# One front phase per layer: opening, norm, 22 projections, low-rank norms, queries, keys and convolution share one phase, and twelve projected tiles pass through memory

## The reference

```python
cond = silu(c)
for l in range(2):
    ada = cond @ ada_w[l] + ada_b[l]              # shift, scale, gate, twice
    h = rms_norm(x, norm1_g[l]) * (1 + sc1) + sh1
    (a_b, a_c, a_x, m_cq, m_ckv, m_kr, s_u, s_v,
     r_q, r_k, r_v, r_g, gate_logits) = split(h @ w_in[l])
    # short conv:  a_b * causal_conv3(a_c * a_x)
    # attention:   q = rms(m_cq) @ w_uq, k,v = rms(m_ckv) @ w_ukv, k_rope = m_kr,
    #              q,k rms-normed per head and rotated; 4 heads of 96, causal softmax
    # spatial gating: gelu(s_u) * (tril(w_s) @ rms(gelu(s_v)) + b_s)
    # retention:   chunked, q,k rotated, silu(r_g) * head_norm(o)
    x = x + g1 * (sum_n sigmoid(gate_n) * (y_n @ w_branch[n])) @ w_o[l]
    h = rms_norm(x, norm2_g[l]) * (1 + sc2) + sh2
    x = x + g2 * channel_mixer(h)
```

## Time and profile before

| what | value |
| --- | --- |
| median of 3 runs | 6089.78 us (6085.6 to 6098.41) |
| profiled execution: time | 6089.61 us |
| profiled execution: span | 6087.8 us |
| busy share of the span: PE, PEld, DVE, ACT, POOL | 89%, 74%, 39%, 30%, 30% |
| mean granted clock of PE | 0.937 |

### The profile page before, as it was taken

How to read it: one execution, slowest core, us unless ns; L and a number is a source line. 1 busy time by engine, 2 the same in 40 slices (tenths; PEclk the granted TensorE clock), 3 DMA queues, 4 the chain that set the end, 5 groups by cost and what they waited for, 6 DMA issues and landing times. The chain is left out here.

```text
span 6087.8 us, 73881 instructions
## 1 busy us (share of the span) xinstructions
PE 5410.3 (89%) x29832; PEld 4520.1 (74%) x29833; DVE 2375.2 (39%) x2058; ACT 1834.3 (30%) x1499; POOL 1846.6 (30%) x506
## 2 busy tenths in 40 slices
PE   6788799979999887978998499999999999999995
PEld 4366577758777663746776498998989898898985
DVE  4453333322422535341111233433364335753356
ACT  2131111123222112211111133333354334643344
POOL 1311011114343322111111152342454254642533
PEclk8798899989999997989999599999999999999997
DMA  4000133323633710101112265555577557975568
GB/s 160 18 19 24 47 80 83 98 62 96 171 109 99 211 35 0 38 4 43 47 45 85 101 210 186 195 191 186 193 257 247 193 182 234 337 254 189 188 226 293
DMA packets 803244, 827.43 MB, mean 136 GB/s; under 512 B 18370, under 2 KB 731202, under 8 KB 802754
## 3 DMA queue, kind: packets, MB, share of 16 engines
q1 hardware_dynamic: 795122, 794.49, 40.8%
q0 software_dynamic: 4608, 16.78, 0.8%
q10 hardware_dynamic: 3408, 14.68, 0.6%
HBM read 780.79 MB, written 45.09 MB: 136 GB/s over the span
## 5 line engine op out<-in xcount | busy, mean ns | idle before, releaser
L1935 POOL TENSOR_TENSOR e_w_lo<-e_raw,e_w_hi 128x2048 fp32r<-128x2048 f32 x170 | 1073.2, 6324 | 1478.3 <-ACT e_w_hi L1873 1478.3
L252 POOL TENSOR_TENSOR w_lo<-w_raw,w_hi 128x1024 fp32r<-128x1024 f32 (+1 forms) x260 | 622.5, 2395 | 2349.7 <-ACT w_hi L247 2349.7
L258 PE MATMUL banks<-e_x_hi,e_w_hi 128*128 128x256 f32 x3584 | 1019.6, 284 | 35.0 <-issue 23.9
L259 PE MATMUL banks<-e_x_lo,e_w_hi 128*128 128x256 f32 x3584 | 1018.5, 284 | 0.0
L260 PE MATMUL banks<-e_x_hi,e_w_lo 128*128 128x256 f32 x3584 | 1018.4, 284 | 0.0
L271 PE MATMUL banks<-h_hi,w_hi 128*128 128x512 f32 x1984 | 806.0, 406 | 127.0 <-POOL w_lo L252 78.5
L1873 ACT ACTIVATE e_w_hi<-e_raw 128x2048 fp32r<-128x2048 f32 x340 | 648.5, 1912 | 541.4 <-PE banks L260 530.2
L272 PE MATMUL banks<-h_lo,w_hi 128*128 128x512 f32 x1984 | 777.9, 392 | 0.0
L258 PEld LDWEIGHTS banks<-e_x_hi,e_w_hi 128*128 128x128 f32 x3584 | 692.7, 193 | 38.3 <-issue 26.0
L259 PEld LDWEIGHTS banks<-e_x_lo,e_w_hi 128*128 128x128 f32 x3584 | 692.6, 193 | 0.0
L260 PEld LDWEIGHTS banks<-e_x_hi,e_w_lo 128*128 128x128 f32 x3584 | 692.4, 193 | 0.0
(11 more groups left out here) (298 smaller groups left out, 7884.1 us busy)
## 6 DMA issues: line engine op xcount, KB each, us to landing
e_raw<-in_moe_w_dram SPq DMA_DIRECT2D x510, 1024.0 KB, 5.1
w_raw<-in_ffn_w_dram SPq DMA_DIRECT2D x120, 512.0 KB, 3.9
w_raw<-in_w_in_dram SPq DMA_DIRECT2D x108, 512.0 KB, 4.1
f_ada_raw<-in_ada_w_dram SPq DMA_DIRECT2D x48, 512.0 KB, 4.7
g_ada_raw<-in_ada_w_dram SPq DMA_DIRECT2D x32, 512.0 KB, 3.8
e_io<-row_scratch SPq DMA_DIRECT2D x13, 1024.0 KB, 6.2
x_scratch<-x_res SPq DMA_DIRECT2D x24, 512.0 KB, 3.2
y_scratch<-e_io ACTq DMA_DIRECT2D x12, 1024.0 KB, 4.2
```

Of the source, the lines that this page charges most:

```text
L252: pool.tensor_tensor(m.w_lo[b][:, 0:kt, :], m.w_raw[b][:, 0:kt, :], m.w_hi[b][:, 0:kt, :].bitcast(F32), ALU.subtract).then_inc(s.lo_ready, 1)
L258: pe.matmul(out, wh, rh, start=first, stop=False)
L259: pe.matmul(out, wh, rl, start=False, stop=False)
L1935: eng.tensor_tensor(flat(w_lo[u]), flat(raw[n % RING]), flat(w_hi[u]).bitcast(F32), ALU.subtract).then_inc(lo_sem[u % 2], 1)
```

## The change

Steps 1 to 5 and step 7 become one `front_phase` per layer. What it does:

- **Order of blocks.** The low-rank q, kv and rope blocks come first (0 to 3), then the 12 blocks of spatial gating and retention (4 to 15), then C, X, B of the convolution twice (16 to 21). Blocks 0 and 1 are done half by half (`half_block`), from block 2 on both halves use PSUM banks 0 and 1, and each half is evicted by itself.
- **Between the halves.** PE has a step (`beside`) after each half of blocks 3 to 11: the low-rank norm at block 3, and for head n, at blocks 4+2n and 5+2n, up, sums, spread, rotation. ACT, DVE and POOL have the matching pieces between their roundings, evictions and rests.
- **Memory.** Blocks 4 to 15 are evicted to a stage of two tiles, and SP stores each to `row_scratch` (12 stores of 512 KB). `attention_phase` loads ten of them back into `m.z` while the heads are worked on, `sgu_phase` the last two.
- **Convolution.** Its products read PSUM directly on DVE (`evict` of blocks 16 to 21) and `convolve` runs on DVE; POOL has no part in it.
- **Norm.** Scale, rounding and rest are on 128x512 halves, 16 rounds of each, and the second half's reciprocal comes between rounds 7 and 8.
- **Opening.** The first set of rotation angles is worked out by DVE before the `ada` work; its sines are taken by ACT after the ninth transposing step; `part_sum` has four buffers and the weight tiles three. The second set comes at blocks 2 to 5.
- **Layer 1.** The loads of x are the phase's first DMAs; the weights, parameters and tables follow, and DVE's first scale also waits for the tables.

```diff
+def half_block(pe, m, b, half, bank, ready=None):
+    tok = slice(half * HALF, (half + 1) * HALF)
+    for k in range(KT):
+        if ready is not None:
+            pe.wait_ge(ready, KT * half + k + 1)
+        last = mm3(pe, m.ps[:, bank, :], m.w_hi[b][:, k, :], m.w_lo[b][:, k, :],
+                   m.h_hi[:, k, tok], m.h_lo[:, k, tok], k == 0, k == KT - 1)
+    return last
+FRONT = ([C_CQ, C_CQ + P, C_CKV, C_KR + QKR - P] + [C_SU + P * i for i in range(12)]
+         + [c + P * t for t in range(2) for c in (C_C, C_X, C_B)])
+# sync
+            def spill(j):
+                sp.wait_ge(s.evicted, ended(j, 1))
...
+            if first:
...
+                for j in range(NB):
+                    if j >= 3:
+                        sp.wait_ge(s.added, j - 2)
+                    sp.dma_start(wb[j % 3][:, :, :], w_view(a.ada_w[0], j * W, W)).then_inc((s.ada0, s.ada1, s.ada2)[j % 3], 16)
+                sp.wait_ge(s.reduced, 4)
+            else:
+                for k in range(KT):
...
+                    sp.dma_start(m.x[:, k, :], a.xs[P * k:P * k + P, :]).then_inc(x_in[k % 4], 16)
             for j in range(2):
+                load(j)
...
             if first:
                 for k in range(KT):
+                    sp.wait_ge(s.copied, KT + k + 1)
+                    sp.dma_start(a.xs[P * k:P * (k + 1), :], m.x[:, k, :]).then_inc(s.kept, 16)
+                sp.wait_ge(s.kept, 16 * KT)
+                sp.wait_ge(s.lo, 2 * KT)
+                sp.dma_start(pos_i[1][:, :], a.positions.rearrange("o s -> (o s)").partition_broadcast(P)).then_inc(s.p_in, 16)
+            else:
+                sp.dma_start(m.table[:, :, :], a.tables).then_inc(s.tab_in, 16)
+            for j in range(2, NFRONT):
+                load(j)
+                if SPILL0 <= j - 3 < CONV0:
+                    spill(j - 3)
+# tensor
+            for half in range(NHALF):
+                for j in range(2):
+                    pe.wait_ge(s.lo_ready, j + 1)
+                    half_block(pe, m, j, half, 4 * j + half, s.lo if j == 0 else None).then_inc(s.halves, 1)
...
+            for j in range(2, NFRONT):
+                pe.wait_ge(s.lo_ready, j + 1)
+                for half in range(NHALF):
+                    pe.wait_ge(s.evicted, ended(j - 1 if j > 2 else 0, half))
+                    half_block(pe, m, j % 2, half, half).then_inc(s.halves, 1)
+                    beside(j, half)
+# tensor, in beside(j, half): head n at blocks 4+2n and 5+2n
+                if step == 0:
...
+                        pe.wait_ge(s.sined, 2 * n)
+                    up(n)
+                elif step == 1:
+                    pe.wait_ge(s.q_squared, 2 * n + 2)
+                    sums(n)
+                elif step == 2:
+                    pe.wait_ge(s.q_inv, n + 1)
...
+                else:
+                    rotate(n)
+# scalar
+            for j in range(2, NFRONT):
+                if j + 1 < NFRONT:
+                    round_w(j + 1)
...
+                if j >= HEAD0 and n < NG and (j - HEAD0) % 2 == 0:
+                    head_in(n)
+                    head_root(n)
+# gpsimd
+            for j in range(2, NFRONT):
+                if j + 1 < NFRONT:
+                    rest_w(j + 1)
...
+                    turn(n - 1)
...
+                    cosines(n)
+# vector
+            else:
+                dve.wait_ge(s.root, 1)
+                invert(0)
+                dve.wait_ge(s.tab_in, 16)
+            for n in range(2 * KT):
+                if n == KT:
+                    invert(1)
+                scale(n)
+                if n:
+                    rest(n - 1)
+            rest(2 * KT - 1)
...
+            for j in range(2, NFRONT):
...
+                evict(j, 0)
+                if first and j == 2:
...
+                    angle(1)
...
+                if ahead and (j - HEAD0) % 2 == 1:
+                    head_norm(head)
+                evict(j, 1)
+                if first and j == 2:
+                    fold(1)
...
+                if ahead and (j - HEAD0) % 2 == 0:
+                    dve.wait_ge(s.q_root, head + 1)
+                    dve.reciprocal(inv_rms[:, :], inv_rms[:, :]).then_inc(s.q_inv, 1)
+                if ahead and (j - HEAD0) % 2 == 1:
+                    head_sine(head)
...
+                if j >= CONV0 and (j - CONV0) % 3 == 1:
+                    convolve((j - CONV0) // 3)
 def build(nc, a):
...
-        opening_phase(nc, m, a)
         for l in range(DEPTH):
-            param_phase(nc, m, a, l)
-            norm_project_phase(nc, m, a, l, C_B, 10, C_KR + QKR - P)
-            conv_lora_phase(nc, m, l)
-            qk = qk_phase(nc, m, l)
-            attention_phase(nc, m, l, qk)
-            project_phase(nc, m, a, l, C_SU, 12)
-            sgu_phase(nc, m, l)
+            qk = front_phase(nc, m, a, l)
+            attention_phase(nc, m, a, l, qk)
+            sgu_phase(nc, m, a, l)
             retention_phases(nc, m, l)
```

More of the change, by code:

```diff
@@ L787, in flat @@
     def flat(t):
         return t.rearrange("p a n -> p (a n)")
-    with phase(nc, "up", "rope_in", "q_in", "squared", "summed", "root", "inv", "spread", "normed", "turned",
-               "cosed", "sined", "done") as (block, s):
+    names = ["squared", "totals", "root", "inv", "scaled", "hi", "lo", "raw0", "raw1", "hi_ready", "lo_ready", "halves", "evicted",
+             "st0", "st1", "ws_in", "prm_in", "ws_turned",
+             "l_squared", "l_summed", "l_root", "l_inv", "l_spread", "l_done",
+             "up", "rope_in", "q_in", "q_squared", "q_summed", "q_root", "q_inv", "q_spread", "normed", "q_turned",
+             "cosed", "sined", "done", "acc"]
@@ new lines, in _ @@
+            act.activation(rstd[:, :, :], m.ps[:, 6:8, :], ACT.Sqrt, bias=cst[:, K_EPS:K_EPS + 1], scale=1.0 / D).then_inc(s.root, 1)
+            for j in range(2):
+                round_w(j)
+            for half in range(NHALF):
+                for k in range(KT):
+                    n = KT * half + k
+                    act.wait_ge(s.scaled, n + 1)
+                    act.activation(m.h_hi[:, k, half * HALF:(half + 1) * HALF], tmp[n % 3][:, :], ACT.Identity,
+                                   bias=m.small[:, B + k:B + k + 1]).then_inc(s.hi, 1)
@@ new lines, in _ @@
+            round_w(2)
+            for j in range(2, NFRONT):
+                if j + 1 < NFRONT:
+                    round_w(j + 1)
+                if j == HEAD0 - 1:
+                    act.wait_ge(s.evicted, ended(2, 1))
+                    act.activation(l_sq[:, :, :].rearrange("p t n -> p (t n)"), zt(m, 0, 3), ACT.Square).then_inc(s.l_squared, 1)
+                    act.wait_ge(s.l_summed, 1)
+                    for q, n in ((0, QL), (1, P)):
+                        r = slice(2 * GR * q, 2 * GR * (q + 1))
+                        act.activation(inv_rms[r, :], m.ps[r, 6, :], ACT.Sqrt, bias=cst[r, K_EPS:K_EPS + 1], scale=1.0 / n).then_inc(s.l_root, 1)
+                n = (j - HEAD0) // 2
+                if j >= HEAD0 and n < NG and (j - HEAD0) % 2 == 0:
+                    head_in(n)
+                    head_root(n)
+                if first and j == HEAD0 + 1:
+                    sine(1)
+                    act.wait_ge(s.reduced, 8)
+                    act.dma_start(a.tables, m.table[:, :, :]).then_inc(s.saved, 16)
@@ L853, in _, with chain @@
         @block.vector
         def _(dve):
-            for n in range(NG):
-                dve.tensor_copy(qk[n][R, 1, :], zt(m, 9)[P - QKR:P, :]).then_inc(s.rope_in, 1)
-            for n in range(NG):
-                t = qk[n]
-                dve.wait_ge(s.root, n + 1)
-                dve.reciprocal(rstd[:, :], rstd[:, :]).then_inc(s.inv, 1)
-                dve.wait_ge(s.spread, n + 1)
+            n_chain = 0
+            def chain(ins):
+                nonlocal n_chain
+                n_chain += 1
+                ins.then_inc(s.chained, 1)
+                dve.wait_ge(s.chained, n_chain)
```

776 lines of the change are left out of this document (370 added, 406 removed).

## The result

The changed kernel took 5991.43 us (median of 4 runs, 5989.23 to 5993.41) against 6091.64 for the kernel before on the same chip: a ratio of 0.9835, 95% interval 0.9818 to 0.9852. The direction was right; the gain is 100 us where 198 was forecast, and the time lies 61 us above the range. In the profiled executions the span went from 6087.8 to 5990.8, so 97.0 us are to be explained.

The account below looks back on a forecast made before the run. PE, 89% busy, was taken to bound most stages, leaving gains only where it stops or runs at low clock. Earlier spatial gating, 102.7 us in layer 0 and 95.6 in layer 1, took 198.3 from 6089.6: 5891, range 5868 to 5930.

Parts of the forecast that it names:

- layer 0, first scale at: Opening of layer 0: VectorE's first scale of the norm waits for POOL's rests until 52.6 us.
- extra of a head: Blocks with heads: up, sums, spread and rotation add 10.5 us of PE work a head, 42.1 for four.
- low clock at the rotations: Rotations of the eight heads: clock loss taken as 1 us a head, 8 in all, between 0 and 40.
- cover of the reciprocal: Head chain: PE ends its next half block 1.2 us after DVE's reciprocal, so no wait shows on PE.
- layer 1, gain: Layer 1: spatial gating at 2537.3 against 2632.9, 95.6 us gained.
- The angles cost 0 there, 1 at worst: Opening of layer 0: DVE's 13 angle passes, 16.5 us, end by 23, when the first ada tile lands.
- They fit between evictions: Layer 0 blocks: DVE's second angles, some 16 us in four pieces, fit between evictions and cost nothing.
- The head's matmuls: PE work of a head: up 5.16 us, sums 0.87, spread 1.05, rotation 3.44, together 10.5.
- What follows it is unchanged, and the gain is the sum of the two shifts: After spatial gating's start in each layer nothing changes, so the gain is 102.7 + 95.6 = 198.3 us.
- Start-up is no better: Rival: angles, ada and the shared port leave both norms where they were; 27 + 17 us lost, 5935; chance 0.03.
- cover fails: Rival: each head step is late on another engine; 104 us more, 5995, or partly 5915; chance 0.13.
- Slower: Rival: the whole front stays at 1.2 GHz, 6460, deciding from 36% of that work; chance 0.01, 0.02 with similar losses.

Follow-up runs that it names:

- without the wait: The changed kernel without VectorE's wait for ScalarE's first sine between the two halves of the angles' edges; 5962.85 us, ratio 0.9793 to the kernel before.
- the one that took 5902: The changed kernel without VectorE's wait for the first sine and with 45 unexecuted matmuls ahead of the expert loop on TensorE; 5902.03 us, ratio 0.9693.

## Why the prediction was wrong

Its steps, with gains as the spatial gating's start in each layer:

```
term                                   forecast  measured
layer 0, first scale at                52.6      69.1   (53.4 without the wait)
layer 0, block 4 with the first head   covered   10.5 us late, with 5 of it clock
extra of a head                        10.5      11.8
low clock at the rotations             8         about 7 (half of 13.7 us in three stretches)
cover of the reciprocal                1.2       1.5
attention with its barrier             104.2     103.8 (layer 0), 105.1 (layer 1)
layer 1, gain                          95.6      91.0
all that follows                       0         +65.4
```

- **"The angles cost 0 there, 1 at worst"** is the step that failed in the opening. The prediction summed VectorE's passes (it counts 13, the trace has 14) and took them as one run. The passes did fit: without the wait they ended at 20.8, ahead of the 23 that was forecast. But one wait stands in their midst, for the engine that is last to be free, and what is queued behind it is the chain that sets the first matmul. The first scale was 16.5 us late, 15.7 of them by this wait. The whole diff has the line (the excerpt ahead of the prediction has not); the instructions had been costed and the wait had not.
- **"They fit between evictions"** failed by the same line in block 4: the passes fit, but the wait for a sine that ScalarE makes behind the head's squares, its root and a table load doesn't. A pair of blocks with its head took 179.58 - 135.47 = 44.1 in place of 33.6.
- **The head's matmuls** were right in kind and mis-sized by 1.3 us, 10.6 for eight: up 5.52 for 5.16, rotation 3.79 for 3.44, sums 1.22 for 0.87, spread 1.30 for 1.05. The 0.43 us a record came from rows of matmuls with full 128x128 weights. The 31.7 us that attention of layer 0 came late are so 16.5 + 10.5 + 5.3, within 1 us. In layer 1, the first matmul came 2.5 us ahead of the forecast less layer 0's shift (2060.29 against 2134.2 - 71.4), the blocks took 6.2 longer and attention 0.9: the 4.6 that are short.
- **Cover, stores, loads back, convolution, attention** were right: no wait of TensorE in the blocks of layer 1, and attention within 1 us. The 1 us a head for the clock came out at about 7 us for all eight, but in another form: none at five rotations and 1.7 to 3.4 us at three.
- **"What follows it is unchanged, and the gain is the sum of the two shifts"** is the largest failure, 65 us. The instructions are unchanged, their place is not: the change makes TensorE's program 7.3 blocks of 256 longer ahead of the expert loop, and the loop went from place 141 to 217. No row of the kernel before shows what another place costs; its waits of 2.3 us on "issue" were the only hint. With the loop at a good place in both kernels the change is worth 6090 - 5928 = 162 us. With the needless wait gone too the time is 5902, against the 5891 forecast. The rivals have no such term: the largest part of the miss was not among them.
- **The rivals.** "Start-up is no better" had a chance of 0.03 and was the nearest for layer 0, with another cause than the ones it named; "cover fails" happened in one head of eight, by a wait that it named only as "sines with their table loads on ACT". In "Slower" the share that decides is 35% (198 of 568), not 36; nothing hangs on it.

## What to carry to other kernels

Moving or unrolling code ahead of a large loop can change that loop's time without touching it: here by 65 us in eight waits of 8 to 15 us, where 2 to 8.5 us had been. Compare the waits on "issue" and the packets of the instruction queue before and after any change of program size, and try a second place with unexecuted code before you judge the change. In a run of instructions that is to be hidden, look for the wait inside it first: what is queued behind it costs, not the passes. And in a dense phase a pause of 3.4 us cost about 7.6 here (61 us for eight), most of the rest by the clock that falls after it; 0.9 us under the cover cost nothing that could be told.

## What was unexpected of the hardware

- The place of a loop's code is worth 64 us of 5991 in the changed kernel and 80 of 6090 in the one before, by matmuls that are never executed.
- The loop's length and its place are separate conditions: 200 instructions fewer made the changed kernel 22 us slower at a bad place, and the kernel before 14 us faster at a good one.
- After a pause of 3.4 us the granted clock fell twice, for 3.4 to 6.8 us each, the second time about the end of the narrow rotation matmuls, so that it is mostly the dense half block behind them that pays, and this in each of eight heads. Without any pause a fall shows at three of eight rotations in the changed kernel and at five in the one that took 5902, with the same code there.
